# Two-block transformer in fp32: where the root mean square of the second block's rows is divided out

## The reference

```python
def rms_norm(x, g):
    xf = x.astype(jnp.float32)
    y = xf * lax.rsqrt(jnp.mean(xf * xf, axis=-1, keepdims=True) + EPS)
    return (y * g.astype(jnp.float32)).astype(x.dtype)
...
        hn = rms_norm(x, norm_gains[i, 0])
        if kind == 0:
            m = stick_breaking_attention(hn, sb_w_qkv[j], sb_w_o[j])
        elif kind == 1:
            m = dilated_attention(hn, dil_w_qkv[j], dil_w_o[j], rel_bias)
...
        x = x + rms_norm(m, norm_gains[i, 1])
        f = conv_ffn(rms_norm(x, norm_gains[i, 2]), ffn_w_up[i], ffn_conv_w[i],
                     ffn_conv_b[i], ffn_w_down[i])
        x = x + rms_norm(f, norm_gains[i, 3])
```

## Time and profile before

| | |
|---|---|
| median of three runs | 2476.04 us |
| profiled execution, own time | 2464.55 us |
| its span in the profile | 2463.1 us |
| PE, matmuls busy | 2182.5 us, 89% |
| DVE busy | 1107.0 us, 45% |
| ACT busy | 880.6 us, 36% |
| POOL busy | 143.2 us, 6% |
| mean granted PE clock | 0.947 |

### The profile page before, as it was taken

How to read it: one execution, slowest core, us unless ns; L and a number is a source line. 1 busy time by engine, 2 the same in 40 slices (tenths; PEclk the granted TensorE clock), 3 DMA queues, 4 the chain that set the end, 5 groups by cost and what they waited for, 6 DMA issues and landing times.

```text
span 2463.1 us, 30255 instructions
## 1 busy us (share of the span) xinstructions
PE 2182.5 (89%) x12891; PEld 1588.8 (65%) x12891; DVE 1107.0 (45%) x1602; ACT 880.6 (36%) x1353; POOL 143.2 (6%) x132
## 2 busy tenths in 40 slices
PE   5869977989996999699986999997989996999997
PEld 4534434467774444477764888785867774888785
DVE  4722216656644221435525555434344445555533
ACT  2411113135532112357744333322234354333321
POOL 0311100000000111000001000001100001000000
PEclk9989998999997999799997999998999997999998
DMA  9668854022223775411011222211312201222120
GB/s 401 271 237 322 308 223 168 0 104 104 104 86 156 281 302 207 172 69 69 35 69 39 98 103 103 90 64 69 114 62 98 79 35 68 103 103 103 69 86 35
DMA packets 35017, 320.63 MB, mean 130 GB/s; under 512 B 6671, under 2 KB 7695, under 8 KB 20239
## 3 DMA queue, kind: packets, MB, share of 16 engines
q1 hardware_dynamic: 21736, 285.44, 29.9%
q0 software_dynamic: 10624, 25.71, 3.2%
q10 hardware_dynamic: 2512, 7.41, 0.8%
HBM read 306.93 MB, written 24.19 MB: 134 GB/s over the span
## 4 chain that ended last, share of the span: by engine, by line
PE 74%; DMA 10%; DVE 9%; ACT 5%; issue 1%; SPq 1%; POOL 0%; ACTq 0%; POOLq 0%; DVEq 0%
PE PS L160 70%; DMA ring<-in_wexp 6%; PE PS L697 2%; DMA ring<-in_wmod 1%; DVE work L2041 1%; DMA work<-ys 1%; PE PS L492 1%; DVE work L2001 1%; ACT work L1343 1%; DVE work L1588 1%; DVE XL L2008 1%; DVE RS L1533 1%; DMA tokens<-work 1%; PE PS L944 1%; DMA ring<-in_sbv 0%
## 5 line engine op out<-in xcount | busy, mean ns | idle before, releaser
L160 PE MATMUL PS<-HS,RS 128*128 128x512 f32 x4320 | 993.6, 391 | 26.6 <-DVE sq L1984 16.6
L160 PEld LDWEIGHTS PS<-HS,RS 128*128 128x128 f32 x4320 | 813.4, 189 | 200.0 <-DVE sq L1984 17.2
L1533 DVE TENSOR_TENSOR RS<-ring,RS 128x1024 fp32r<-128x1024 f32 x212 | 257.3, 1221 | 314.4 <-ACT RS L1038 314.4
L160 PE MATMUL PS<-ring,work 128*128 128x512 f32 x768 | 346.4, 601 | 17.9 <-DMA ring<-in_wexp 13.3
L1038 ACT ACTIVATE RS<-ring 128x1024 fp32r<-128x1024 f32 x212 | 222.0, 1053 | 236.1 <-PE PS L160 219.6
L160 PEld LDWEIGHTS PS<-ring,work 128*128 128x128 f32 x768 | 142.7, 192 | 180.3 <-issue 160.5
L1038 ACT ACTIVATE work<-PS 128x384 f32<-128x384 f32 (+2 forms) x254 | 121.2, 512 | 221.9 <-PE PS L160 88.5
L1447 ACT ACTIVATE work<-PS,vec 128x512 f32<-128x512 f32 x88 | 68.5, 779 | 308.2 <-PE PS L160 308.2
L2135 DVE SCALAR_TENSOR_TENSOR work<-PS,vec,work 128x511 f32<-128x511 f32 x88 | 66.0, 750 | 217.5 <-ACT work L1447 217.5
L160 PE MATMUL PS<-work 128*64 128x128 f32 (+5 forms) x1696 | 139.0, 300 | 8.6 <-DVE work L2095 4.4
L160 PEld LDWEIGHTS PS<-work 128*64 128x64 f32 (+2 forms) x1696 | 105.5, 145 | 36.7 <-issue 19.6
(11 more groups left out here) (211 smaller groups left out, 2221.2 us busy)
## 6 DMA issues: line engine op xcount, KB each, us to landing
ring<-in_wexp SPq DMA_DIRECT2D x32, 3072.0 KB, 12.9
ring<-in_wmod SPq DMA_DIRECT2D x24, 2048.0 KB, 12.5
ring<-in_ffnu SPq DMA_DIRECT2D x22, 2048.0 KB, 7.7
ring<-in_ffnd SPq DMA_DIRECT2D x10, 2048.0 KB, 7.2
ring<-in_dilqk SPq DMA_DIRECT2D x6, 2048.0 KB, 7.6
work<-ys SPq DMA_DIRECT2D x10, 1024.0 KB, 7.6
ring<-in_sbqk SPq DMA_DIRECT2D x4, 2048.0 KB, 7.7
ring<-in_dilv SPq DMA_DIRECT2D x3, 2048.0 KB, 8.6
```

The source lines that it names most:

```text
L160: return T.matmul(out, l, r, start=start, stop=stop, skip_group_check=True)
L1533: V.tensor_tensor(lo, src, hi.bitcast(F32), ALU.subtract).then_inc(w_lo, 1)
```

## The change

- Rows go into the projection undivided: ACT makes hi from XL times gain (`hi_parts`), DVE makes lo (`rows_lo`) from XL, gain and hi in one instruction, both chunk by chunk as XL's chunks come. The product is divided afterwards: the spread reciprocal is copied to `RB`; query and key products are multiplied by it as DVE moves them out of PSUM (ACT moved the queries before); the rows' groups are scaled per partition by a column `rcol` as ACT copies them; in the feed-forward DVE first multiplies each product by `RB` into four buffers `hr`, and taps read `hr`.
- PE's order: the projection begins with chunk 0, and the `stat_add`s and the spread lie between its matmuls. `ffn` takes its first two units together, chunk by chunk. In `stick` the transposes of the experts' result also lie between them.
- `transition` takes the place of `add_normed` and `normed` between stages 1 to 4: DVE multiplies, POOL adds all eight chunks, in the order 0, 1, 6, 7, 2, 3, 5, 4.
- ACT squares the last products from PSUM ahead of its copy. The next stream's first two units are split earlier, during the stage before; in front of `stick` the lo parts of three units come ahead of `combine` on DVE. The feed-forward's products lie in banks 4 to 7. In the up phase the taps of unit n-1 stand behind the multiplication of unit n.

```diff
+    stream("ffn0", ffn_units(0), 5, 3, 5, (2, 0, 1, 3, 4), (2, 1, 0, 0, 0))
...
+           [(("dilo", 0), A["dilo"], 4096, by_columns(4, 1024), 4)], 2, 2, 2, None, (4, 3))
+    stream("ffn1", ffn_units(1), 5, 3, 5, (2, 0, 1, 3, 4), (2, 1, 0, 0, 0))
...
+        before = first - over[p - first] if p - first < places else p - places + 1
...
+    ORDER = [tuple(range(8))] + [(0, 1, 6, 7, 2, 3, 5, 4)] * 3
...
+        def combine_turn(c):
+
...
+            pe.wait_ge(cb_y, 10)
+            pe.wait_ge(cb_x, 16 + c - 1)
...
-        def project_rows(first, b0, i):
+        def project_rows(first, b0, i, call=None, turns=((),) * 8):
...
+                    for c in turns[n]:
+                        combine_turn(c)
+                    pe.wait_ge(w_lo, first + q + 1)
+                    pe.wait_ge(nm_l, 8 * i + n + 1)
...
+                    if call:
+                        for m in ((0,), (1, 2), (3, 4), (5, 6), (7,), (), (), ())[n]:
+                            stat_add(call, m)
+                        if n == 5:
+                            pe.wait_ge(st_rcp, call + 1)
+                            if i == 0:
+                                T.transpose(PS[:, 0, 0:128], rs[:, 0, :], ident)
+                            stat_spread(call)
...
         def ffn(i):
-            stat(9 + 4 * i)
+            call, at = 9 + 4 * i, 1 + 2 * i
...
-            for j in range(44):
-                pe.wait_ge(fu_d, 44 * i + j - 3)
-                project(first + j, j % 4, 1 + 2 * i)
+            pair_of = [parts(first + u) for u in range(2)]
+            pe.wait_ge(w_lo, first + 2)
+            for n, k in enumerate(ORDER[at]):
+                pe.wait_ge(nm_l, 8 * at + n + 1)
+                for u, (key, src, hi, lo, before) in enumerate(pair_of):
+                    x = mm3(PS[:, 4 + u, :], (hi[:, k, :], lo[:, k, :]), hs(k), n == 0, n == 7)
+                    if n == 7:
+                        x.then_inc(w_done, 1)
+                if n:
+                    stat_add(call, n - 1)
+            stat_add(call, 7)
...
+            project(first + 2, 6, at, range(4))
+            stat_spread(call)
+            project(first + 2, 6, at, range(4, 8))
+            for j in range(3, 44):
+                pe.wait_ge(fu_r, 44 * i + j - 3)
+                project(first + j, 4 + j % 4, at)
...
-                pe.wait_ge(fu_d, 44 * i + 44)
+                pe.wait_ge(fu_r, 44 * i + 44)
...
-        def hi_parts(i, name):
+        def hi_parts(i, name, late):
...
+            for n, c in enumerate(ORDER[i]):
+                act.wait_ge(*((an_xp, 8 * i - 8 + n + 1) if i else (cb_x, 16 + c + 1)))
+                act.wait_ge(tab_out, 16)
+                copy(rows_out(i, HS[:, c, 0, :]), rows_in(i, XL[:, c, :]), scale=gain(i, c)).then_inc(nm_h, 1)
+                square(call, n, XL[:, c, :], st_add, SEQ[call, n] - 3)
+                if n == 4:
+                    split_hi(name, late[0])
+            split_hi(name, late[1])
             root(call)
+            act.wait_ge(st_bc, call + 1)
+            copy(rows_out(i, RB[i]), rows_in(i, PS[:, 2, :])).then_inc(rb_c, 1)
...
-                copy(dst(t), PS[:, b0 + t, :]).then_inc(pr_c, 1)
...
+                copy(dst(t), PS[:, b0 + t, :], scale=rcol[:, t:t + 1]).then_inc(pr_c, 1)
...
+                square(call, c, PS[:, 4 + c % 2, :], st_add, SEQ[call, c] - 3)
                 copy(HL[:, c, :], PS[:, 4 + c % 2, :]).then_inc(po_c, 1)
-                square(call, c, HL[:, c, :], po_c, po + c + 1)
+                if c == 6:
+                    split_hi(after, part_of[after].start + 2)
             root(call)
+            split_hi(after, part_of[after].start + 3)
...
+        def rows_lo(i, n):
+
+            c = ORDER[i][n]
+            dve.wait_ge(nm_h, 8 * i + n + 1)
+            V.scalar_tensor_tensor(out=rows_out(i, HS[:, c, 1, :]), in0=rows_in(i, XL[:, c, :]), scalar=gain(i, c),
+                                   in1=rows_out(i, HS[:, c, 0, :].bitcast(F32)), op0=ALU.mult,
+                                   op1=ALU.subtract).then_inc(nm_l, 1)
...
+                if layer == 1 and c > 1:
+                    rows_lo(0, c - 2)
...
+        def transition(a, name, late):
+
+            rcp(8 + 2 * a)
+            split_lo(name, part_of[name].start + (2 if a == 1 else 3))
+            dve.wait_ge(st_bc, 9 + 2 * a)
+            dve.wait_ge(*((fd_ca, 4) if a == 1 else (po_c, 4 * a + 8)))
+            for n, c in enumerate(ORDER[a + 1]):
+                if n > 3:
+                    dve.wait_ge(an_xp, 8 * a + n - 3)
+                g = ((0, 1), (0, 3), (1, 1))[a]
+                V.scalar_tensor_tensor(out=W(13312 + n % 4 * 512, 512), in0=HL[:, c, :],
+                                       scalar=VC("ng", (g[0] * 4 + g[1]) * 8 + c, 1),
+                                       in1=PS[:, 2, :], op0=ALU.mult, op1=ALU.mult).then_inc(an_t, 1)
+                if n > 1:
+                    rows_lo(a + 1, n - 2)
+                if n == 6:
+                    split_lo(name, late[0])
+            rows_lo(a + 1, 6)
+            rows_lo(a + 1, 7)
+            split_lo(name, late[1])
+            rcp(9 + 2 * a)
 
...
+                V.scalar_tensor_tensor(out=s_q[j % 2], in0=PS[:, 6, :], scalar=0.125, in1=RB[0], op0=ALU.mult,
+                                       op1=ALU.mult).then_inc(sk_q, 1)
...
-                dve.wait_ge(sk_z, 2 * (j - 1))
-                V.tensor_copy(s_k[j % 2], PS[:, 7, :]).then_inc(sk_k, 1)
+                V.tensor_tensor(s_k[j % 2], PS[:, 7, :], RB[0], ALU.mult).then_inc(sk_k, 1)
...
+            def taps(n):
+                j, s = n // 2, n % 2
+                y, ch = gu[j % 2][s], 22 * s + j
+                dve.wait_ge(fu_a, 44 * i + n + 1)
+                step(V.scalar_tensor_tensor(out=y[:, 1:512], in0=hr[n % 4][:, 0:511], in1=y[:, 1:512], op0=ALU.mult,
+                                            scalar=VC("convw", (i * 3 + 1) * 44 + ch, 1), op1=ALU.add))
+                V.scalar_tensor_tensor(out=y[:, 2:512], in0=hr[n % 4][:, 0:510], scalar=VC("convw", i * 3 * 44 + ch, 1),
+                                       in1=y[:, 2:512], op0=ALU.mult, op1=ALU.add).then_inc(fu_d, 1)
...
+            for n in range(44):
+                split_lo(name, ahead(name, n))
+                dve.wait_ge(rb_c, 2 + 2 * i)
+                dve.wait_ge(w_done, first + n + 1)
+                dve.wait_ge(fu_a, 44 * i + n - 3)
+                V.tensor_tensor(hr[n % 4], PS[:, 4 + n % 4, :], RB[1 + 2 * i], ALU.mult).then_inc(fu_r, 1)
+                if n:
+                    taps(n - 1)
+                if n > 2 and n % 2:
+                    gated(n // 2 - 1)
+            taps(43)
+            gated(21)
...
+        split_lo("stick", ahead("stick", 0))
         combine(1, 4)
```

More of the change, by code:

```diff
@@ L238, in build, with stream @@
     UNIT, STREAM, part_of = [], {}, {}
-    def stream(name, units, places, early, later=None):
+    def stream(name, units, places, early, later=None, order=None, over=()):
         first = len(UNIT)
-        STREAM[name] = (first, places, early, later or early)
+        STREAM[name] = (first, places, early, later or early, order or range(places), over or (0,) * places)
         for key, src, n, cut, many in units:
@@ L597, in combine @@
                     x.then_inc(cb_t, 1)
+        def combine_turn(c):
+            pe.wait_ge(tb_c, 6)
+            pe.wait_ge(mo_xd, 32)
+            pe.wait_ge(cb_y, 10)
+            pe.wait_ge(cb_x, 16 + c - 1)
+            for t in range(4):
+                x = T.transpose(PS[:, (c % 2) * 2 + 1, t * 128:(t + 1) * 128], pair[:, t, 0, c * 128:(c + 1) * 128], ident)
+            x.then_inc(cb_t, 1)
         def tables():
@@ L1389, in project_qk @@
                 rot = 16 * j - 4 if j else 0
-                for g in range(3):
-                    i = 2 * g
+                for i in range(6):
                     split_hi("dil", ahead("dil", 12 + 6 * j + i))
-                    act.wait_ge(w_done, first + 12 + 6 * j + i + 1)
-                    act.wait_ge(sm_s, 64 + 8 * j)
-                    copy(blocks(d_q[:, g, :]), blocks(PS[:, TURN[(rot + i) % 3], :])[:, :, ::-1], scale=0.125).then_inc(dq, 1)
-                    split_hi("dil", ahead("dil", 12 + 6 * j + i + 1))
             def powers(u, h):
@@ L1433, in dilated @@
             act.wait_ge(sm_b, 32)
-            project_out("dil", 36, 4, 8, 12)
-            split_hi("ffn1", ahead("ffn1", 0, False))
+            project_out("dil", 36, 4, 8, 12, "ffn1")
         def ffn(i):
@@ L1463, in ffn @@
                 split_hi(name, ahead(name, 44 + k))
+            if i == 0:
+                split_hi("dil", ahead("dil", 0))
             table(0)
@@ L2122, in dilated @@
                 split_lo("dil", ahead("dil", 36 + c // 2))
-            add_normed(2, "ffn1")
+            split_lo("ffn1", part_of["ffn1"].start + 2)
+            transition(2, "ffn1", (0, part_of["ffn1"].start + 4))
         def ffn(i):
@@ L2154, in ffn @@
                 split_lo(name, ahead(name, 44 + k))
```

(2 more changed lines are left out.)

240 lines of the change are left out of this document (98 added, 142 removed).

## The result

Four runs of the changed kernel took 2436.2, 2438.6, 2448.5 and 2450.3 us, a median of 2443.5. The kernel before ran a fourth time beside them (2471.2 us), which makes its median 2473.6: a ratio of 0.9875 (95% interval 0.9835 to 0.9915). The forecast was 2438.2. The profiled execution had 2436.19 us, a span of 2434.7, which is 28.4 us less than the span before.

What follows compares the result with a forecast made beforehand. PE was taken as the bound within stages, with gains where it stands still. 17.3 + 20.1 + 10.7 - 5.3 - 5.0 = 37.8 us off the 2476.04 median gave 2438.2 us, range 2425 to 2454.

Steps and rivals of the forecast that it cites:

- What bounds: Whole kernel: PE bounds each stage, spare DVE and ACT time is worth nothing, and gains lie where PE stands still.
- ffn0, 17.3: Change of stage from stick to ffn0: first two units done at 1326.3 instead of 1343.65, a gain of 17.3 us.
- slow start: Behind each pause PE starts at its lower clock, costing 2.2 us at ffn0, 2.5 at stick.
- ffn1, 20.1: Change of stage into ffn1: first units and spread done at 2068.6 against 2088.7, a gain of 20.1 us.
- dil, 10.7: Change of stage into dil: PE-bound first group ends at 1736.3 against 1747.03, a gain of 10.7 us.
- stick, -5.3: Head of stick: additions wait behind lo parts that wait for weights; first group ends at 1048.8 against 1043.48, 5.3 us lost.
- Up to down, -2.5 twice: Between up and down: DVE's work behind the last matmul grows 2.05 us, slow start perhaps 0.4; 2.5 us lost, twice.
- The lock: Changes of stage: two-SBUF-input DVE instructions and SBUF-reading POOL instructions exclude each other; without it four changes end some 2 us sooner.
- the high bound: Time of `rows_lo` beside POOL: POOL's whole instruction plus 0.55 us, chosen over the low 0.69.
- PE starving at the start: Rival at feed-forward starts: DVE's multiplication also waits for POOL, period 2.8 us, gain 27, total 2449 us; chance 0.10.
- the ring of DVE and ACT: Slower rival: a DVE-ACT ring of 9.1 us per unit pair bounds the up phase if links lengthen, 2495 us; chance 0.03.
- the low clock: Rival: PE stays at the low clock while fed in pieces, 9 us in each feed-forward, 2456 us; chance 0.06.

Runs made afterwards that it cites:

- Run 7: Changed kernel, but DVE makes two of the four scaled copies of the last row group ahead of dilated attention, where ACT made all four; one time, 2426.4 us.
- run 3: Changed kernel, but DVE instead of POOL does the additions to XL in the three changes of stage; median 2443.7 us, ratio 0.9893.
- run 11: Changed kernel with the four edits, plus result-free filling matmuls on PE at its waits around ffn0, ffn1, dil and down; median 2417.5 us, ratio 0.9787.
- both series of the changed kernel: The changed kernel unedited, measured twice: first four runs, median 2443.5 us; later again beside its edits, median 2431.3 us.
- the four edits: Changed kernel plus late lo parts before stick, chunk 3's transposes first, early taps ending up phases, two scaled copies by DVE; medians 2425.1 and 2424.6 us.

## Why the prediction was right, and where it was not

- **What bounds** was right: the gain came where PE stood, 35.4 us of it at the two feed-forwards for 37.4 forecast, and DVE's 154.8 busy us in the 229.7 of an up phase (127.8 in 236.9 before) cost nothing.
- **ffn0, 17.3 against 17.5**, but by errors that cancel. The pause was 7.79 us for 8.5, since the spread took 1.16 us at the high clock; the forecast's 1304.95 for DVE's first multiplication is reached only with the 1.89 that it took at this place before (the row below). The slow start cost 1.9 us (12 matmuls in 4.62) for 2.5. Against these, a chunk on PE was mis-sized: 1.94 us for 1.72. "The next matmul starts 0.36 after" a `stat_add` is true, but the term needed is what the whole adds to 6 matmuls, 0.58; the earlier trace rows has nearly that: from the `stat_add` at 2036.20 to the end of the 12 matmuls behind it are 3.37 us, 0.65 over their 2.72. All eight `stat_add`s together cost 4.0 us for 2.9.

```profile
1303.64 1.89 PE L160 MATMUL PS<-rs,cst 128*128 128x128 f32 x8 [1.48 <-DVE rs L1566]
```

- **ffn1, 20.1 against 17.9.** The `stat_add`s again (4.1 for 2.9), a slow start of 2.7 us (12 matmuls in 5.44) for 2.5, a pause of 8.43 for 8.2; and before the change the slow start had cost 1.7 here (13 matmuls in 4.67), not the 2.2 that the forecast takes over from ffn0.
- **dil, 10.7 against 9.2** from the reciprocal to the end of the first group (8.4 us from reciprocal to PE, 6.7 forecast): the spread ran at the low clock (1.84 us for 1.2), the strided hi took 1.21 us where 0.6 was taken, and the first strided lo part 2.03 us beside POOL. (From the end of the spread, as in the table, the gain is 9.9.) Then 2.0 us were given back at the scaled copies, 0.36 by a longer wait and 1.6 by the clock behind it; the prediction does not price them at all. Run 7 shows them. This is the step that was missing.
- **stick, -5.3 against -3.3.** Order and waits came as written, L1882 at 1011.82, 4.5 us behind the landing of the weights for 4.7; the slow start (2.5) was nearly absent in that execution (the first 12 matmuls took 3.00 us), but not in others: the head took 71.3 to 74.7 us in the seven profiles of this order.
- **Up to down, -2.5 twice against -2.7 and -2.3.** Right; 0.65 of the -2.7 is the slow spread ahead of dil, already counted there.
- **The lock** was right (run 3), and so was the choice of the high bound: the lo parts end 0.55 us behind POOL, as DVE's addition did in the earlier trace rows. Of the rivals, PE starving at the start did not come, but run 11 shows it next in line; the ring of DVE and ACT did not form, with 5.44 us a unit; the low clock lasted longer than before in ffn1 alone.
- The range held both series of the changed kernel (2443.5 and 2431.3). The spread of 8 us that it was built on was too small: the four runs of the first series lie 14 apart.

## What to carry to other kernels

A normalization that is a factor for each row can be divided out of a projection's result, and what it buys is the time in which the matrix engine would have waited for the sum. Cost then every small consumer that gets the factor in its place: a copy that becomes 0.09 us longer, four times in a row ahead of a waiting PE, gave back a fifth of one change's gain. When the pauses are short, matmuls that do nothing can be worth as much as a finer order on the other engines (7.1 us for run 11's, 6.7 for the four edits), as long as they end just when the rows are ready.

## What the runs showed of the hardware

- PE's clock did not fall behind a wait of 2.20 us and fell behind one of 2.56 at the same place in all eight profiles that have it (the stretch behind it 39.94 to 40.01 us, 38.35 before), but behind waits of 2.57 us in the dilated attention only sometimes. In run 11 it was low again behind a wait of 1.90 us, with the clock raised just ahead of it. So no length of a wait by itself tells whether the clock falls.
- The first 12 matmuls at the head of stick took 3.0 to 5.2 us in the seven profiles of one order, by where the low clock ended. A forecast of a slow start has that spread in it.
